# State space scan: the skip term added on VectorE in token order, the tiles normalised on GpSimd and turned by transpositions

## The reference

```
xbc = silu(causal_conv(x @ w_in[z-part excluded]))        # xs, b_in, c_in
dt  = softplus(dt_raw + dt_bias);  a = -exp(a_log)
y   = ssd_chunked_scan(xs, dt, a, b_in, c_in) + xs * d_skip[head]
y   = y * silu(z)
yg  = y.reshape(bsz, s, 4 groups, 512)
yg  = yg * rsqrt(mean(yg**2, -1) + 1e-5)
y   = (yg.reshape(...) * norm_w) @ w_out
```

## Time and profile before

| | |
|---|---|
| runs | 4629.28, 4641.80, 4650.21 us; median 4641.8 |
| profiled execution | 4639.03 us, its span from first to last instruction 4637.3 us |
| mean granted TensorE clock | 0.916 of full speed |
| projections of this layer | 2215.5 to 2516.4 us of the span |
| scan, items | 2516.4 to about 2641 us |
| scan, tail of turned tiles | to 2660.4 us |

### The profile page before, as it was taken

One profiled execution on the slowest core, in us unless ns is written; L12 is line 12 of the kernel. 1 busy time (PEld: TensorE's weight loads), 2 busy tenths in 40 slices (PEclk: granted clock), 3 DMA queues, 4 the chain that ended last, 5 costly groups with the idle time before them and its releaser, 6 DMA issues. The chain is left out here.

```text
span 4637.3 us, 60067 instructions
## 1 busy us (share of the span) xinstructions
PE 3867.4 (83%) x24647; PEld 2647.9 (57%) x24647; DVE 1687.0 (36%) x3008; ACT 707.6 (15%) x1510; POOL 822.8 (18%) x667
## 2 busy tenths in 40 slices
PE   4989978999898888999999895877749887677773
PEld 2478856884446757874458744444439864444441
DVE  6667745630375653211431512000052343200003
ACT  2211112110231221100212500000020132000000
POOL 1122214330100214420100110000034332000001
PEclk9989999999899989999999896999969877798997
DMA  3221313633121012221121017999922100899995
GB/s 119 73 83 48 120 60 121 225 109 113 35 66 47 2 42 82 82 104 55 57 74 53 14 68 289 399 403 407 411 84 83 55 1 20 320 384 389 399 396 210
DMA packets 252360, 707.56 MB, mean 153 GB/s; under 512 B 22284, under 2 KB 136404, under 8 KB 201460
## 3 DMA queue, kind: packets, MB, share of 16 engines
q1 hardware_dynamic: 234660, 662.04, 38.6%
q10 hardware_dynamic: 12880, 25.72, 1.5%
q0 software_dynamic: 4608, 16.78, 0.9%
HBM read 667.24 MB, written 37.24 MB: 152 GB/s over the span
## 5 line engine op out<-in xcount | busy, mean ns | idle before, releaser
L3219 PE MATMUL experts_pg<-moe_wg,experts_xt 128*64 128x256 f32 x4224 | 528.9, 414 | 130.8 <-DMA moe_wg<-in_moe_w_up 112.4
L3219 PEld LDWEIGHTS experts_pg<-moe_wg,experts_xt 128*64 128x64 f32 x4224 | 332.9, 150 | 309.8 <-issue 165.8
L3234 PE MATMUL experts_py<-moe_wd,experts_ht 128*64 128x512 f32 x1056 | 261.5, 640 | 41.6 <-DVE experts_ht L3286 24.1
L534 PE MATMUL ffn_out_y<-ffn_out_ring,ffn_h 128*128 128x512 f32 x640 | 275.7, 592 | 0.0
L3284 DVE TENSOR_TENSOR experts_h<-experts_hs,experts_pg 128x256 f32<-128x256 f32 x66 | 27.8, 421 | 647.2 <-ACT experts_hs L3253 647.2
L611 PE MATMUL ffn_in_seven<-ffn_in_seven_t,ffn_in_seven_s 128*128 128x256 f32 x1056 | 236.7, 381 | 0.0
L3313 POOL DMA_INDIRECT merge_yg<-y_rows,moe_yi x16 | 16.1, 1005 | 1144.0 <-PEq L3302 596.0
L611 PEld LDWEIGHTS ffn_in_seven<-ffn_in_seven_t,ffn_in_seven_s 128*128 128x128 f32 x1056 | 202.0, 191 | 28.1
L534 PEld LDWEIGHTS ffn_out_y<-ffn_out_ring,ffn_h 128*128 128x128 f32 x640 | 121.3, 190 | 151.1 <-issue 151.1
L3234 PEld LDWEIGHTS experts_py<-moe_wd,experts_ht 128*64 128x64 f32 x1056 | 83.0, 145 | 174.5 <-issue 174.5
L3280 DVE COPY experts_xt<-experts_px 128x512 f32<-128x512 f32 x66 | 45.7, 692 | 333.4 <-PE experts_px L3211 333.4
(11 more groups left out here) (697 smaller groups left out, 6676.0 us busy)
## 6 DMA issues: line engine op xcount, KB each, us to landing
moe_wg<-in_moe_w_gate SPq DMA_DIRECT2D x66, 2048.0 KB, 20.4
moe_wg<-in_moe_w_up SPq DMA_DIRECT2D x66, 2048.0 KB, 24.9
moe_wd<-in_moe_w_down SPq DMA_DIRECT2D x66, 2048.0 KB, 25.7
ffn_in_ring<-in_ffn_w_in SPq DMA_DIRECT2D x42, 1024.0 KB, 5.3
ffn_in_ada_ring<-in_ada_w SPq DMA_DIRECT2D x28, 1024.0 KB, 6.6
ffn_out_ring<-in_ffn_w_out SPq DMA_DIRECT2D x20, 1024.0 KB, 5.2
ssd_proj_ring<-in_ssd_w_in SPq DMA_DIRECT2D x19, 1024.0 KB, 5.3
att_kqt<-in_attn_w_qkv SPq DMA_DIRECT2D x17, 1024.0 KB, 5.1
```

The source lines that it names most:

```text
L534: last = nc.tensor.matmul(y[:, tt, half, :], h[:, kk, tt * P:(tt + 1) * P], ring[n][:, q, half * BANK:(half + 1) * BANK], start=(kk == 0), ...
L3219: last = nc.tensor.matmul(pg[ch * SLOTS:(ch + 1) * SLOTS, b, side, 0:HH], xt[:, b, kk % MQ, kk // MQ, :], wg[:, b, side, kk, ch * HH:(ch + ...
L3234: last = nc.tensor.matmul(py[half * SLOTS:(half + 1) * SLOTS, b, :], ht[:, b, kk % HM, kk // HM, :], wd[:, b, kk, half * HALF:(half + 1) * ...
```

## The change

1. In the projections GpSimd's multiplication of the x tiles by d and the column `d_col` go. VectorE reads the turned tile a second time, multiplies it by d per head and writes it over `feat[:, m, :]`, now in token order: row = token, and 128 features of the tile beside each other for each of the 4 token tiles.
2. In the scan the four identity products per item go; y's sum starts with the products m times xdt, and the wait for `y_taken` moves to just before them. VectorE adds the item's part of `feat` to yv after L2644, with a wait for L2644's end before it and for its own end after it.
3. `diagonals` becomes `inverses`: the reciprocal alone. GpSimd multiplies z's tile by it, in place, one scalar per token (`normal(n - 5)`, after the state's decay in item n; the last five after the loop), and TensorE turns the tile by four transpositions with the identity in place of four products with the diagonal.

```diff
@@ projections
-                    @block.gpsimd
-                    def _(pool):
-                        pool.wait_ge(s["d_done"], 2)
-                        for m in range(X_TILES):
-                            pool.wait_ge(s["turn_made"], m + 1)
-                            nc.gpsimd.tensor_tensor(feat[:, m, :], feat[:, m, :], d_col[:, m:m + 1].to_broadcast([P, T]), ALU.mult).then_inc(s["scaled"], 1)
-                        pool.wait_ge(s["scaled"], X_TILES)
...
-                        by_head = d_row[:, :].rearrange("p (m a) -> p m a", a=2)
-                        for half in range(2):
-                            part = slice(half * 64, (half + 1) * 64)
-                            nc.vector.tensor_copy(d_col[part, 0:X_TILES], by_head[part, :, half]).then_inc(s["d_done"], 1)
...
-                                nc.vector.tensor_tensor(xdt[...], turned[...], dt[...], ALU.mult).then_inc(s["x_taken"], 1)
+                                by_head = turned[:, m % 2, :].rearrange("p (t h n) -> p t h n", t=TT, h=2)
+                                nc.vector.tensor_tensor(xdt[...], by_head, dt[...], ALU.mult).then_inc(s["x_made"], 1)
+                                nc.vector.tensor_tensor(feat[:, m, :].rearrange("p (t h n) -> p t h n", t=TT, h=2), by_head,
+                                                        d_row[:, 2 * m:2 * m + 2].unsqueeze(1).unsqueeze(3).to_broadcast([P, TT, 2, HP]),
+                                                        ALU.mult).then_inc(s["x_taken"], 1)
+                        dve.wait_ge(s["x_made"], X_TILES)
@@ scan, GpSimd
+                def normal(pool, n):
+                    c, g, _ = item(n)
+                    zs = z[:, c, g * GW:(g + 1) * GW]
+                    pool.wait_ge(s["inverse_done"], c + 1)
+                    nc.gpsimd.tensor_scalar(zs, zs, ss[:, c % 2, g:g + 1], None, ALU.mult).then_inc(s["normal_done"], 1)
...
+                            if n >= LAG:
+                                normal(pool, n - LAG)
+                        for n in range(ITEMS - LAG, ITEMS):
+                            normal(pool, n)
@@ scan, TensorE
-                            pe.wait_ge(s["diag_done"], c + 1)
+                            pe.wait_ge(s["normal_done"], n + 1)
...
-                                last = nc.tensor.matmul(tp[:, q, :], z[:, c, g * GW + q * P:g * GW + (q + 1) * P], diag[:, c % 2, g, :], start=True, stop=True)
+                                last = nc.tensor.transpose(tp[:, q, :], z[:, c, g * GW + q * P:g * GW + (q + 1) * P], k.ident[:, :])
...
-                            if n >= 2:
-                                pe.wait_ge(s["y_taken"], n - 1)
-                            for q in range(4):
-                                nc.tensor.matmul(y[:, b, q * P:(q + 1) * P], feat[:, g * 4 + q, t], k.ident[:, :], start=(q == 0), stop=False,
-                                                 skip_group_check=True)
...
+                            if n >= 2:
+                                pe.wait_ge(s["y_taken"], n - 1)
                             pe.wait_ge(s["m_done"], n + 1)
                             for e in range(E):
-                                                        start=False, stop=(e == E - 1), skip_group_check=True)
+                                                        start=(e == 0), stop=(e == E - 1), skip_group_check=True)
@@ scan, VectorE
                         def norms(c):
+                            if c >= 2:
+                                dve.wait_ge(s["normal_done"], G * (c - 1))
...
-                        def diagonals(c):
+                        def inverses(c):
                             dve.wait_ge(s["root_done"], c + 1)
-                            step(nc.vector.reciprocal(ss[:, b, :], ss[:, b, :]))
-                            if c >= 2:
-                                dve.wait_ge(s["tp_made"], G * (c - 1))
-                            nc.vector.tensor_tensor(diag[:, b, :, :], ...ident..., ss[:, b, :].unsqueeze(2).to_broadcast([P, G, P]), ALU.mult).then_inc(s["diag_done"], 1)
+                            nc.vector.reciprocal(ss[:, b, :], ss[:, b, :]).then_inc(s["inverse_done"], 1)
...
                             nc.vector.tensor_tensor(e2(yv[:, :]), e2(off[:, :]), e_cs[...], ALU.mult).then_inc(s["off_taken"], 1)
+                            dve.wait_ge(s["off_taken"], n + 1)
+                            q4 = yv[:, :].rearrange("p (q n) -> p q n", q=4)
+                            step(nc.vector.tensor_tensor(q4, q4, feat[:, g * 4:(g + 1) * 4, c * CH:(c + 1) * CH], ALU.add))
                             dve.wait_ge(s["ds_made"], n + 1)
```

More of the change, by code:

```diff
@@ L2317, in ssd_stages @@
                 small = st.sb("small", [P, DK, H])
-                dt_row, alog_row, d_row, d_col = (st.sb(n, [P, H]) for n in ("dt_row", "alog_row", "d_row", "d_col"))
+                dt_row, alog_row, d_row = (st.sb(n, [P, H]) for n in ("dt_row", "alog_row", "d_row"))
                 sp_ = Softplus(st, "softplus", [P, TT, H])
@@ L2322, in ssd_stages @@
                 names = ("small_in", "rows_in", "small_made", "alog_done", "da_done", "sums_done", "arg_done", "exp_done", "made", "raw_done",
-                         "conv_done", "silu_done", "tok_taken", "zeroed", "dve_step", "turn_made", "x_taken", "b_taken", "d_done", "scaled")
+                         "conv_done", "silu_done", "tok_taken", "zeroed", "dve_step", "turn_made", "x_made", "x_taken", "b_taken")
                 s = {n: st.sem(n) for n in names}
@@ L2465, in _ @@
                                 dve.wait_ge(s["turn_made"], m + 1)
-                                nc.vector.tensor_tensor(xdt[:, :, m * P:(m + 1) * P].rearrange("p t (h n) -> p t h n", h=2),
-                                                        turned[:, m % 2, :].rearrange("p (t h n) -> p t h n", t=TT, h=2),
-                                                        dt[:, :, 2 * m:2 * m + 2].unsqueeze(3).to_broadcast([P, TT, 2, HP]), ALU.mult).then_inc(s["x_taken"], 1)
+                                by_head = turned[:, m % 2, :].rearrange("p (t h n) -> p t h n", t=TT, h=2)
+                                nc.vector.tensor_tensor(xdt[:, :, m * P:(m + 1) * P].rearrange("p t (h n) -> p t h n", h=2), by_head,
+                                                        dt[:, :, 2 * m:2 * m + 2].unsqueeze(3).to_broadcast([P, TT, 2, HP]), ALU.mult).then_inc(s["x_made"], 1)
+                                nc.vector.tensor_tensor(feat[:, m, :].rearrange("p (t h n) -> p t h n", t=TT, h=2), by_head,
+                                                        d_row[:, 2 * m:2 * m + 2].unsqueeze(1).unsqueeze(3).to_broadcast([P, TT, 2, HP]),
+                                                        ALU.mult).then_inc(s["x_taken"], 1)
+                        dve.wait_ge(s["x_made"], X_TILES)
                         dve.wait_ge(s["x_taken"], X_TILES)
@@ L2474, in ssd_stages @@
                 xrest, dec, m = st.sb("xrest", [P, 2, E, HP]), st.sb("dec", [P, 2, E, P]), st.sb("m", [P, 2, E, P])
-                yv, diag = st.sb("yv", [P, GW]), st.sb("diag", [P, 2, G, P])
+                yv = st.sb("yv", [P, GW])
                 stats, mv, ss = st.sb("stats", [P, 2, G, 6]), st.sb("mv", [P, 2, G, 2]), st.sb("ss", [P, 2, G])
@@ L2479, in ssd_stages @@
                 names = ("zeroed", "rest_done", "decayed", "gb_made", "relu_done", "exp_done", "cb_made", "cb_masked", "m_done", "off_made", "ds_made",
-                         "y_made", "off_taken", "state_done", "y_taken", "gated", "var_done", "root_done", "diag_done", "tp_made", "tp_taken", "dve_step")
+                         "y_made", "off_taken", "state_done", "y_taken", "gated", "var_done", "root_done", "inverse_done", "normal_done", "tp_made", "tp_taken", "dve_step")
                 s = {n: st.sem(n) for n in names}
@@ L2624, in norms @@
                             nc.vector.scalar_tensor_tensor(ss[:, b, :], ss[:, b, :], SSD_EPS, mv[:, b, :, 1], ALU.add, ALU.add).then_inc(s["var_done"], 1)
-                        def diagonals(c):
+                        def inverses(c):
                             b = c % 2
                             dve.wait_ge(s["root_done"], c + 1)
-                            step(nc.vector.reciprocal(ss[:, b, :], ss[:, b, :]))
-                            if c >= 2:
-                                dve.wait_ge(s["tp_made"], G * (c - 1))
-                            nc.vector.tensor_tensor(diag[:, b, :, :], k.ident[:, :].rearrange("p (a t) -> p a t", a=1).to_broadcast([P, G, P]),
-                                                    ss[:, b, :].unsqueeze(2).to_broadcast([P, G, P]), ALU.mult).then_inc(s["diag_done"], 1)
+                            nc.vector.reciprocal(ss[:, b, :], ss[:, b, :]).then_inc(s["inverse_done"], 1)
                         dve.wait_ge(s["zeroed"], 1)
@@ L2656, in _ @@
                             if n % G == 0 and n:
-                                diagonals(c - 1)
+                                inverses(c - 1)
```

(2 more changed lines are left out.)

## The result

The changed kernel takes 4656.4 us (median of 20 runs, 4646.5 to 4673.9) against 4641.9 for the kernel before (20 runs, 4626.9 to 4658.7). The ratio is 1.0035, its 95% interval 1.0024 to 1.0046: slower by 14.6 us, which is more than chance and less than the 0.5% that the prediction called a difference. The forecast was 4660.

The account below looks back on a forecast made before the run. A closed ring between VectorE and TensorE bounds the scan, TensorE the projections. Ring +14.7, tail -3.2 and clock +8 sum to +19.5 on the profiled 4639.0, so 4658.5; forecast median 4660 us, range 4638 to 4691.

Parts of the forecast that it names:

- ring: Scan: closed loop gate of n-1, m of n, y of n, gate of n; 15 steps from 115.1 to 129.8 us, +14.7.
- tail: After the scan's items: four turns through one tp buffer fall from 3.37 to 2.4 us, normalisation costs +0.7; -3.2 us.
- clock: Scan: larger TensorE gaps ahead of y bring five more falls to the low clock, 1.7 us each, +8 us.
- Projections at nothing: Projections: 16 added VectorE products, 11.0 us, cost nothing, covered by TensorE's 299.4 of 300.9 us.
- the addition's +0.83: Scan, VectorE: the addition and its waits between L2644 and L2649 lengthen each step by 0.83, from 6.69 to 7.52 us.
- The port: Scan: GpSimd's normalisation holds up VectorE's addition through the shared port, +0.87 a step, to 8.39 us.
- rival 1: Scan: the addition alone costs, no port delay, clock stays; ring 123.1 us, +8.0, less 3.2: 4647 us; chance 0.2.
- Boundaries: Scan steps at a chunk's boundary: from 10.14 us to 9.8 at the first and 10.97 at the other two.
- chain: Scan: the added instruction waiting for results on both sides in VectorE's ring, +0.83 us per step.
- TensorE at the low clock for most of the scan: Rival 2, scan: TensorE's half-speed work of 11.4 us per item sets the step; 4689 us; chance 0.15.
- TensorE's relief: Rival 3, scan: the 19.4 us of work TensorE no longer does is gained, plus 3.2 of tail; 4619 us; chance 0.05.

Follow-up runs that it names:

- gaps filled: The changed kernel plus six products per item that nobody reads, in TensorE's gap ahead of y; 4647.9 us, ratio 0.9996 to 1.0022 to the kernel before.
- skip term alone: The changed kernel with the diagonals and the products with them put back, so without the new normalisation; 4663.8 us, ratio 1.0031 to 1.0066 to the kernel before.
- m first: The changed kernel with VectorE making m of item n ahead of the gate of n-1; 4611.6 us, ratio 0.9946 to the kernel before.

## Why the prediction came true, and where it did not

**The forecast was close, its terms less so.** 4660 was 3.6 above the median. But the sum behind it was +19.5 (ring 14.7, tail -3.2, clock 8), and the stage gave +12.0.

- *Projections at nothing*: held. 300.9 us, VectorE 86.9 busy. I had expected about 100: the 16 new products came, and L2450 (median 1.17 us; L2438 in the changed kernel, 0.49) no longer stretched beside GpSimd's products. Off the path either way.
- *The ring and the addition's +0.83*: held. L2642 to L2650 is 1.45, the step 7.60 (7.52 forecast). Over the 12 steps that cross no boundary this is 91.2 against 84.6 before, +6.6 (5.6 by the forecast's 7.52). Moving the addition behind m (6.82) and leaving it out (6.75) both undo it, by no more than its place.
- *The port, "+0.87 … Steps with normalisation become 8.39"*: failed. It was to bring 9 x 0.87 = 7.8 us; the 12 steps lost 1.0 to it. I took L2623's row beside a decay, a product of two tensors, as the rule for any GpSimd instruction. The experiments show that the form decides: beside the two-tensor product the addition waits (7.86 measured, 7.93 was my figure for that price), beside the multiplication by a scalar it waits only if it starts within that one's first half microsecond, and not even then where both begin together. So the forecast's addition of 1.4 to 1.6 us from item 5 on came twice (1.52 and 1.59), both times beside xrest. My rival 1 had the steps right, but for a reason that I had not written down; it gave 123.1 for the ring (with 10.97 at all three boundaries, where the forecast had 9.8 at the first), and 130.4 came, because of the next two points.
- *Boundaries*: 9.8, 10.97 and 10.97 forecast, 11.02, 10.30 and 12.40 measured, +3.2 over before in place of +1.3. All three meet the low clock. In the first it reached L2613 by way of ScalarE's late square root, 1.1 us, a path that I had left out; an addition of 0.91 beside xrest added 0.2. In the second VectorE waited for nothing up to m, and L2626 took 1.00 beside the decay; whether the low clock brought those two together is not shown. The last holds y at 3.65 us and a wait of L2613 for it of 3.74, and an addition of 1.59 beside xrest.
- *The clock*: five more falls were forecast and five came, longer ones (30.4 us together, in which half speed could cost 15), and the tail's fall began some 5 us before the ring's end. The steps that cross no boundary paid 4.5 us for all of these, 1.7 of it in the last step, since part of each lies in work that has time; 8 was forecast. What the boundaries paid is in their +3.2. With the gaps filled the first boundary took 10.11 at full clock in place of 11.02; for the other two no run parts it from the rest.
- *Tail*: held, -3.05 for -3.2, turn 2.41 for 2.4, normalisation 1.56 for 1.5.

Measured, the terms are chain +6.6, port +1.0, clock in the same 12 steps +4.5, boundaries +3.2, tail -3.05, head -0.2: 12.0. Against the sum, the port brought 6.8 less and the clock 3.5 less, the boundaries 2.0 and the chain 1.0 more. So the step that failed is the port's. That the end came out within 3.6 us is in part luck: the sum was 7.5 us above the stage's +12.0, the forecast was rounded 1.3 us below the median plus the sum (4641.8 + 19.5 = 4661.3), and the medians differ by 2.6 more than the stage does. Those 2.6 are not explained; runs of one kernel differ by more.

**The rivals.** TensorE at the low clock for most of the scan did not come: some 35 of 130 us of the ring. The Trainium skill (TensorE: Matmul & The Clock Gate, Part 4: PE-mode transpose) has it that a transposition doesn't count for the clock as a product does. The runs don't bear it out as a cause here: the skip term alone turns by products, and its ring has eight low stretches; in the changed kernel the clock fell in the first chunk too, where nothing is turned; and without the addition two of the six low stretches were left with all transpositions in place. TensorE's relief came through in full only where the ring was cut (m first), which is the condition that this rival had named; with the addition out of the ring's way it gave some 0.3 us a step (7.08 to 6.75 or 6.82).

**The price from a page.** The Trainium skill (GPSIMD Engine Reference, Elementwise side-by-side cycle accounting) has 769 ns as the best case for 512 elements; the row shows 1560 ns for this form, so the price scaled from the row for 768 elements (1.47) was the better one. The Trainium skill (SBUF — State Buffer, SBUF: two separate sides) also has it that the port shared by the two engines is locked for the whole instruction. For the product of two tensors these traces agree within 0.14 us; for the scalar form they do not, by a whole microsecond.

## What to carry to other kernels

When an engine's idle time sits in a closed ring with another engine, new work on it is free only behind the instruction that releases the other: the same addition cost 0.85 us a step ahead of m and 0.07 behind it. Cut the ring first (m before the gate), then move work off the busy engine; in the other order the same change loses what it would gain. And take a price for interference from a row of the same form of instruction, not only of the same engine.

## What the runs showed of the hardware

- GpSimd's multiplication of 128x512 by a per-row scalar takes 1.56 us, a product of two tensors 1.04. Yet the former holds up a VectorE instruction with two SBUF inputs only for about its first 0.54 us: a VectorE product of four elements (L2625, 2629.30, 0.53) ended 0.70 us after a normalisation's start (2629.13), of which 0.16 is its own work, and the addition at 2606.21 gives the same 0.54. The product of two tensors holds it until 0.14 us of its end.
- The wait can fall on the other engine. Where L2615 (0.69, two inputs in SBUF) was under way, it was GpSimd's instruction that grew: a normalisation of 2.01 (2569.54) and a decay of 1.35 (2586.37) in place of 1.56 and 1.04. The same where a normalisation and an addition began within 0.03 us of each other: 2.07 for the one, 0.69 for the other. Off the path, such a wait cost nothing. The wait shows as a longer instruction, not as idle time ahead of it.
- Gaps of 1.4 to 2 us ahead of y in most steps, some longer ones at the boundaries, went with six low stretches in the ring; gaps of 0.6 or less in the ordinary steps behind the first chunk (filled gaps, no addition, addition behind m), with 1.8 to 2.9 at the boundaries, went with two; and with m first, where TensorE is busy 97.3 of 103.0 us, the granted clock stayed at 1.00.
